# Value products with the values stationary, probabilities divided before they are turned, and a compression in four quadrants

## Chip, core and metric

The kernel runs on one core of a Trainium2 chip. The metric is the device time in microseconds of one launch, the median of three runs; lower is better. The engines are called PE (TensorE), DVE (VectorE), ACT (ScalarE), POOL (GpSimd) and SP (SyncE, which issues the DMAs).

## What is computed

Two transformer blocks on 256 tokens of width 1024, in float32. The change touches the mixer of the first block alone. It projects the tokens, runs three kinds of attention with 4 heads of 64 columns each, and merges them through gates:

```
o_a = stick_breaking(q_a, k_a, v_a)               # w from a suffix sum; o = w @ v, nothing divided
o_b = dsa(q_b, k_b, v_b, index heads)             # o = softmax(scores of chosen keys) @ v_b
kc  = silu(blocks_of_32(k_cmp) @ w1_k) @ w2_k     # 15 blocks of 32 tokens, step 16; vc alike
o_c = g0 * (softmax(q_c kc) @ vc) + g1 * (softmax_sel @ v_sel) + g2 * (softmax_win @ v_win)
merged = sum_j g[j] * (o_j @ w_up[j]);  out = merged @ w_out
```

(silu stands for the gating function of the hidden layer.) The softmax is divided by its sum; whether the division comes before or behind the product with the values is free.

## The kernel before

**Blocks.** The large products run in weight blocks of 256 columns: one DMA of 1 MB into one of four raw buffers, then ACT rounds it to a high part (L1406, "cast", called hi here), DVE subtracts to get the low part (L1742, lo), and PE runs 48 matmuls of 128x128 by 256 (L786 to L788) in two halves of 24. The gate blocks' results are taken from PSUM by DVE (L1753) and then go through a tanh on ACT (L1422), both called the evacuation. The first mixer's blocks are proj 0 to 8, gate 0 to 11, up 0, 2, 1 and out 0 to 3, in that order.

**Order.** Each engine runs a list of steps in one order, written out by hand in `plan()`. A step stands in it once, and each engine that has a part in it does its part at that place of its own row. `between` puts steps between the two halves of a block's matmuls; `evac` comes behind the block and behind the hi and lo of a block that lies two ahead (`ahead`), so DVE evacuates a gate block after it has written another block's lo. Engines meet by semaphores: `fill` tells that a PSUM bank is written, `free` that it is read, and `claim` makes PE wait for a free bank.

**The steps in question.** Units 4 to 11 are the heads of c (query tile t, head h; selected and window keys are two parts of one unit), units 0 to 3 pairs of heads of b. For each, `scores` has PE write logits, DVE mask and take the maximum, and ACT take exponentials and sums (L1593); `turn_p` has PE transpose the probabilities (L1249) and ACT copy them (L1608); `pv` (L1272) multiplies them with the probabilities stationary and 64 value columns moving. `pv_stick` (L1131 to L1133) does so for the stick heads, `cmp_pv` (L1206) for the compressed keys. `o_group` on DVE divides the results and, for c, weighs and adds them (L2134, L2167 to L2195); `turn_o` has PE transpose them (L1286) and ACT and DVE write their high and low parts for the up blocks. `cmp_product` (L1169) is the first layer of the compression: 16 products of a 128-row piece by 16 columns, in two steps of 8 for keys and two for values; `cmp_hidden` on DVE (L2047) and ACT (L1560) is what follows.

**Merging.** After an up block, `merge` on DVE (L2222) weighs its quarter, POOL adds branches (L1691), and `merged_hi`, `merged_lo` (L1631, L2233) split the sum for out 0.

## Time and profile before

| what | us |
|---|---|
| runs | 751.66, 754.02, 752.17 |
| median of the runs | 752.17 |
| span of the profiled execution | 750.7 |

The rows below come from that one profiled execution, whose span is 1.5 us under the median; all times of day in it count from the span's start. The busy time of a group of matmuls ends with the tail of its last one, so the distance between starts is shorter than the busy time divided by the count. A float32 matmul is two instructions.

### The profile page before, as it was taken

The page shows a single profiled execution, that of the slowest core. Times are in us where ns is not written, and L with a number is a line of the kernel's source. Part 1 is how long each engine was busy: PE and PEld are TensorE (multiplying, and loading weights), DVE is VectorE, ACT ScalarE, POOL GpSimd, SP SyncE. Part 2 cuts the span into 40 slices and gives each one's busy share as a digit, 9 for nine tenths or more (in the row PEclk, how much of TensorE's full clock was granted, in tenths as well). Part 3 has the DMA queues.
Part 4 walks back from the last instruction along what each step waited for, and adds up shares of the span by engine and source line. Part 5 has one row for each costly group of instructions (what it writes and reads, how often), then busy time and mean ns, then how long its engine had stood idle before and what let it go on. Part 6 is the DMA issues. An engine that isn't in the chain of part 4 may idle for free.

```text
span 750.7 us, 15016 instructions
## 1 busy us (share of the span) xinstructions
PE 742.7 (99%) x6374; PEld 733.2 (98%) x6374; DVE 601.2 (80%) x897; ACT 376.9 (50%) x506; POOL 30.6 (4%) x22
## 2 busy tenths in 40 slices
PE   8999999999999999999999999999999999999998
PEld 8999999999999999999999999999999999999997
DVE  5756889889897788998998788979787886687554
ACT  6558255745676533443434547356556553434330
POOL 0000000004000000000000000201110000000000
PEclk9999999999999999999999999999999999999999
DMA  9844373342843459999987336655344565678511
GB/s 336 319 153 146 110 275 113 113 139 108 309 174 115 169 173 389 334 349 329 335 306 271 138 127 230 224 174 219 103 173 139 205 224 173 224 281 301 201 58 56
DMA packets 24113, 156.07 MB, mean 208 GB/s; under 512 B 3568, under 2 KB 3696, under 8 KB 6000
## 3 DMA queue, kind: packets, MB, share of 16 engines
q1 hardware_dynamic: 24048, 155.13, 57.6%
q8 instruction: 50, 0.82, 0.4%
q14 instruction: 15, 0.12, 0.0%
HBM read 154.07 MB, written 1.05 MB: 207 GB/s over the span
## 4 chain that ended last, share of the span: by engine, by line
PE 95%; DVE 2%; ACT 1%; DMA 1%; issue 1%; DVEq 0%; SPq 0%
PE bank L786 17%; PE bank L787 16%; PE bank L788 16%; PE bank L867 9%; PE bank L870 9%; PE bank L869 9%; PE bank L794 3%; PE bank L796 3%; PE bank L797 3%; PE bank L1272 2%; PE bank L1239 1%; PE bank L1249 1%; PE bank L1169 1%; DMA sb_raw<-in_stream 1%; PE bank L1322 0%
## 5 line engine op out<-in xcount | busy, mean ns | idle before, releaser
L1742 DVE TENSOR_TENSOR sb_lo<-sb_raw,sb_hi 128x2048 fp32r<-128x2048 f32 (+1 forms) x116 | 261.7, 2259 | 74.5 <-ACT sb_hi L1406 74.1
L1406 ACT CAST sb_hi<-sb_raw 128x2048 fp32r<-128x2048 f32 (+1 forms) x116 | 217.8, 1882 | 100.7 <-PE bank L870 49.3
L786 PE MATMUL bank<-sb_u_hi,sb_hi 128*128 128x256 f32 (+2 forms) x696 | 195.4, 281 | 0.0
L787 PE MATMUL bank<-sb_u_lo,sb_hi 128*128 128x256 f32 (+2 forms) x696 | 192.7, 277 | 0.0
L788 PE MATMUL bank<-sb_u_hi,sb_lo 128*128 128x256 f32 (+2 forms) x696 | 192.6, 277 | 0.0
L786 PEld LDWEIGHTS bank<-sb_u_hi,sb_hi 128*128 128x128 f32 (+2 forms) x696 | 129.6, 186 | 3.0 <-issue 2.2
L787 PEld LDWEIGHTS bank<-sb_u_lo,sb_hi 128*128 128x128 f32 (+2 forms) x696 | 129.8, 186 | 0.3
L788 PEld LDWEIGHTS bank<-sb_u_hi,sb_lo 128*128 128x128 f32 (+2 forms) x696 | 129.7, 186 | 0.2
L867 PE MATMUL bank<-sb_hid_hi,sb_hi 128*128 128x256 f32 x432 | 119.3, 276 | 0.0
L870 PE MATMUL bank<-sb_hid_hi,sb_lo 128*128 128x256 f32 x432 | 119.2, 276 | 0.0
L869 PE MATMUL bank<-sb_hid_lo,sb_hi 128*128 128x256 f32 x432 | 119.2, 276 | 0.0
L786 PE MATMUL bank<-sb_hi,sb_u_hi 128*128 128x256 f32 x320 | 90.9, 284 | 0.0
L787 PE MATMUL bank<-sb_lo,sb_u_hi 128*128 128x256 f32 x320 | 88.8, 277 | 0.0
L788 PE MATMUL bank<-sb_hi,sb_u_lo 128*128 128x256 f32 x320 | 88.8, 277 | 0.0
L869 PEld LDWEIGHTS bank<-sb_hid_lo,sb_hi 128*128 128x128 f32 x432 | 81.1, 188 | 0.0
L867 PEld LDWEIGHTS bank<-sb_hid_hi,sb_hi 128*128 128x128 f32 x432 | 81.1, 188 | 0.0
L870 PEld LDWEIGHTS bank<-sb_hid_hi,sb_lo 128*128 128x128 f32 x432 | 81.1, 188 | 0.0
L786 PEld LDWEIGHTS bank<-sb_hi,sb_u_hi 128*128 128x128 f32 x320 | 60.3, 188 | 0.2
L787 PEld LDWEIGHTS bank<-sb_lo,sb_u_hi 128*128 128x128 f32 x320 | 60.2, 188 | 0.1
L788 PEld LDWEIGHTS bank<-sb_hi,sb_u_lo 128*128 128x128 f32 x320 | 60.1, 188 | 0.0
L2269 DVE SCALAR_TENSOR_TENSOR sb_raw<-sb_raw,sb_c_row 128x1024 f32<-128x1024 f32 x48 | 56.7, 1219 | 0.0
L1444 ACT ACTIVATE sb_act_out<-sb_masked 128x256 f32<-128x256 f32 x22 | 9.1, 418 | 81.8 <-DVE sb_masked L1822 81.8
(368 smaller groups left out, 1330.3 us busy)
## 6 DMA issues: line engine op xcount, KB each, us to landing
sb_raw<-in_stream SPq DMA_DIRECT2D x140, 1024.0 KB, 5.2
sb_raw<-in_stream SPq DMA_DIRECT2D x4, 256.0 KB, 6.6
sb_raw<-in_stream SPq DMA_DIRECT2D x2, 512.0 KB, 8.5
sb_mem_t<-in_mem SPq DMA_DIRECT2D x1, 1024.0 KB, 4.8
out<-sb_h SPq DMA_DIRECT2D x4, 256.0 KB, 2.2
sb_const<-in_constants SPq DMA_DIRECT2D x1, 830.0 KB, 10.8
sb_h<-in_x SPq DMA_DIRECT2D x1, 572.0 KB, 3.6
sb_h<-in_x SPq DMA_DIRECT2D x1, 512.0 KB, 7.0
```

Source lines behind the costliest of these rows:

```text
L786: nc.tensor.matmul(out, a_hi, b_hi, start=(i == 0), stop=False)
L787: nc.tensor.matmul(out, a_hi, b_lo, start=False, stop=False)
L788: last = nc.tensor.matmul(out, a_lo, b_hi, start=False, stop=(i == n - 1))
L794: nc.tensor.matmul(out, a_hi, b_hi, start=(k == 0 and i in opens), stop=False, skip_group_check=True)
L796: nc.tensor.matmul(out, a_hi, b_lo, start=False, stop=False, skip_group_check=True)
L797: last = nc.tensor.matmul(out, a_lo, b_hi, start=False, stop=(k == KD - 1), skip_group_check=True)
L867: nc.tensor.matmul(out, w_hi[:, k, f], x1, start=(first and k == m == 0), stop=False, skip_group_check=True)
L869: nc.tensor.matmul(out, w_hi[:, k, f], x2, start=False, stop=False, skip_group_check=True)
L870: last = nc.tensor.matmul(out, w_lo[:, k, f], x1, start=False, stop=last_one and k == 1, skip_group_check=True)
L1406: nc.scalar.copy(place(hi, s)[:, 0:n], x[:, 0:n]).then_inc(sem("hi_ready"), 1)
L1742: tt(place(lo, s)[:, 0:n], x[:, 0:n], f32(place(hi, s)[:, 0:n]), ALU.subtract) \
L2269: ins = stt(x[:, m, :], x[:, m, :], 1.0, c_row[:, :], ALU.mult, ALU.mult, accum_out=mod[:, 2 * j + m:2 * j + m + 1])
```

## The change

1. Value products (`pv_pair`, `pv_stick`, `cmp_pv`) have 64 value columns stationary and the probabilities moving, two heads in the two column halves of the array. The result is already the transposed output, and `turn_o` on PE goes.
2. Since rows of that result are no longer queries, the division moves ahead: `norm_p` has POOL raise the sums to the power -1 (for c times the gates) and ACT scale each head's probabilities, before `turn_p`. For the compressed keys `turn_cmp_p` on DVE divides. `o_group` for these groups goes.
3. `cmp_product` runs its 16 products in four quadrants of 32 columns with the piece of tokens stationary; ACT copies the result to `cmp_parts`, and `cmp_sum` adds the four with one product by a constant, `pick`, in the middle of the gate block where the second half of the products stood.
4. `turn_o` 0 is taken in gate 2 instead of ahead of gate 6, `turn_o` 2 ahead of up 0, `turn_o` 1 within up 0.

```diff
-    block("gate", 2, between=[("pv_stick", 3), ("o_group", 0), ("turn_cmp", 1), ("index", 0), ("rope1", 3)])
-    steps([("cmp_product", 0, 0)])
-    block("gate", 3, between=[("cmp_product", 0, 1), ("cmp_hidden", 0), ("topk", 0, 0)])
-    steps([("cmp_product", 1, 0), ("topk", 0, 1), ("turn_qk", 2)])
+    block("gate", 2, between=[("pv_stick", 2), ("turn_o", 0), ("turn_cmp", 1), ("index", 0), ("rope1", 3)])
+    steps([("cmp_product", 0)])
+    block("gate", 3, between=[("cmp_sum", 0), ("cmp_hidden", 0), ("topk", 0, 0)])
+    steps([("cmp_product", 1), ("topk", 0, 1), ("turn_qk", 2)])
...
-    steps([("turn_p", 6), ("turn_p", 7), ("scores", 8), ("scores", 9), ("topk", 1, 1), ("split", "gate", 9)])
-    block("gate", 8, ahead=False, evac_now=False, between=[("cmp_pv",), ("o_group", 1)])
+    steps([("turn_p", 6), ("turn_p", 7), ("scores", 8), ("scores", 9), ("norm_p", 8), ("norm_p", 9), ("topk", 1, 1), ("split", "gate", 9)])
+    block("gate", 8, ahead=False, evac_now=False, between=[("cmp_pv",)])
...
     evac(where["gate", 11])
+    add("turn_o", 2)
     split(where["up", 2])
...
+                for k in range(16):
+                    r = slice(32 * (k % 4), 32 * (k % 4) + 32)
+                    pair = 16 * (k - k % 2)
+                    last = nc.tensor.matmul(ps[r, 0:P], cmp_in[:, i, pair:pair + 32], w[:, k, :], start=(k < 4),
+                                            stop=(k >= 12), skip_group_check=True)
+                fill(last, key)
+
+            def cmp_sum(i):
+
+                wait_evacuated(pe, ("cmp_parts", i))
+                ps = claim(("cmp_hidden", i), "turn")
+                fill(nc.tensor.matmul(ps[:, 0:16], cmp_parts[:, i, :], cst("pick"), start=True, stop=True),
+                     ("cmp_hidden", i))
...
+                    for x in (u, u + 1):
+                        i = UNITS[x][2]
+                        r = slice(HD * (i % 2), HD * (i % 2) + HD)
...
+                            out = ps[r, i // 2 * T + t * P:i // 2 * T + t * P + P]
+                            v, p = proj[:, kt, (VSEL, VWIN)[s]:(VSEL, VWIN)[s] + HD], p[:, s, kt, :]
+                        last = nc.tensor.matmul(out, v, p, start=(opens and n == 0), stop=(n == len(parts) - 1),
+                                                skip_group_check=True)
...
+            def cmp_product(i):
+
+                key = ("cmp_parts", i)
+                ps = wait_filled(act, key)
+                free(nc.scalar.copy(cmp_parts[:, i, :], ps[:, 0:P]), key)
...
+            def norm_p(u):
+
+                n = P * (UNITS[u][1] + 1)
+                act.wait_ge(sem("rden_ready"), EXP_ORDER[u] - 3)
+                for m in range(2):
+                    x = prob_of(u)[:, m * n:m * n + n]
+                    last = nc.scalar.activation(x, x, ACT.Copy, scale=rden[:, u, m:m + 1])
+                last.then_inc(sem("p_ready"), 1)
...
+            def norm_p(u):
+
+                pool.wait_ge(sem("exp_done"), EXP_ORDER[u] + 1)
+                kind, t, h = UNITS[u]
+                if kind == "c":
+                    pool.wait_ge(sem("gate_c_halved"), 1)
+                r = rden[:, u, :]
+                ins = nc.gpsimd.tensor_tensor(r, den[:, u, :], minus_one[:, :], ALU.pow)
+                if kind == "c":
+                    link(ins)
+                    ins = nc.gpsimd.tensor_tensor(r, r, gate_c[:, t, h, 1:3], ALU.mult)
+                ins.then_inc(sem("rden_ready"), 1)
...
+                heads = p.rearrange("p (h n) -> p h n", n=32)
+                tt(heads, heads, over(cmp_d[:, :], 32), ALU.mult).then_inc(sem("cmp_p_ready"), 1)
```

The first place is ACT's row around gates 2 to 4, before: the tanh of gate 1 (`sb_gates`), casts, the tanh of gate 2, the hidden unit's tanh (`sb_hid_t`).

```order
L1422 ACTIVATE sb_gates<-sb_gates 128x512
L1406 CAST sb_hi<-sb_raw 128x2048 x2
L1422 ACTIVATE sb_gates<-sb_gates 128x512
L1560 ACTIVATE sb_hid_t<-sb_hid_t 128x15
L1406 CAST sb_hi<-sb_raw 128x2048
L1422 ACTIVATE sb_gates<-sb_gates 128x512
L1529 COPY sb_qk_t<-bank 128x512
L1560 ACTIVATE sb_hid_t<-sb_hid_t 128x15
L1406 CAST sb_hi<-sb_raw 128x2048
```

The same place after:

```order
L1664 ACTIVATE sb_turned_hi<-bank 128x512
L1435 CAST sb_hi<-sb_raw 128x2048
L1451 ACTIVATE sb_gates<-sb_gates 128x512
L1590 COPY sb_prob_t<-bank 128x128
L1595 ACTIVATE sb_hid_t<-sb_hid_t 128x15
L1435 CAST sb_hi<-sb_raw 128x2048
L1451 ACTIVATE sb_gates<-sb_gates 128x512
L1590 COPY sb_prob_t<-bank 128x128
L1558 COPY sb_qk_t<-bank 128x512
L1595 ACTIVATE sb_hid_t<-sb_hid_t 128x15
```

A copy of 128x128 out of PSUM, the partial sums of the compression (`cmp_parts`, kept in `sb_prob_t`), now follows the tanh of gate 2 and another one the tanh of gate 3; the high part of output 0 (`sb_turned_hi`) stands between two casts.

PE waits for that copy. Its row in the middle of gate 3 (the gate's own matmuls are `sb_u_hi`, `sb_u_lo`), before:

```order
L787 MATMUL bank<-sb_u_lo,sb_hi 128x256
L788 MATMUL bank<-sb_u_hi,sb_lo 128x256
L1169 MATMUL bank<-sb_cmp_in,sb_raw 128x16 x8
L786 MATMUL bank<-sb_u_hi,sb_hi 128x256
L787 MATMUL bank<-sb_u_lo,sb_hi 128x256
L788 MATMUL bank<-sb_u_hi,sb_lo 128x256
```

And after:

```order
L790 MATMUL bank<-sb_u_lo,sb_hi 128x256
L791 MATMUL bank<-sb_u_hi,sb_lo 128x256
L1185 MATMUL bank<-sb_const,sb_prob_t 128x16
L789 MATMUL bank<-sb_u_hi,sb_hi 128x256
L790 MATMUL bank<-sb_u_lo,sb_hi 128x256
L791 MATMUL bank<-sb_u_hi,sb_lo 128x256
```

Instead of 8 products of the compression, whose operands are long there, one matmul stands that reads the copy.

The second place is ACT's row around the exponentials of heads 8 and 9 (128x256 x4) and the casts of gates 9 and 10 behind them, before:

```order
L1608 COPY sb_prob_t<-bank 128x256 x2
L1593 ACTIVATE sb_prob,sb_den<-sb_masked,sb_neg_max 128x256 x4
L1406 CAST sb_hi<-sb_raw 128x2048 x2
L1608 COPY sb_prob_t<-bank 128x512 x2
L1593 ACTIVATE sb_prob,sb_den<-sb_masked,sb_neg_max 128x256 x4
L1422 ACTIVATE sb_gates<-sb_gates 128x512
L1406 CAST sb_hi<-sb_raw 128x2048
```

And after:

```order
L1643 COPY sb_prob_t<-bank 128x256 x2
L1628 ACTIVATE sb_prob,sb_den<-sb_masked,sb_neg_max 128x256 x4
L1656 ACTIVATE sb_prob<-sb_prob,sb_rden 128x256 x4
L1435 CAST sb_hi<-sb_raw 128x2048 x2
L1643 COPY sb_prob_t<-bank 128x512 x2
L1628 ACTIVATE sb_prob,sb_den<-sb_masked,sb_neg_max 128x256 x4
L1656 ACTIVATE sb_prob<-sb_prob,sb_rden 128x256 x4
```

Four scalings that need POOL's inverse now stand between the exponentials and the casts, and again ahead of the tanh.

## Rows read from the trace of the kernel before

**Rows 1.** The page's shares of the span: engine, busy us, share, instructions.

```profile
PE 742.7 (99%) x6374; PEld 733.2 (98%) x6374; DVE 601.2 (80%) x897; ACT 376.9 (50%) x506; POOL 30.6 (4%) x22
```

**Rows 2.** Waits of PE (40 to 190 us) and DVE (96 to 190): total, times, longest.

```profile
PE bank L867 <- issue: 0.2, 1, 0.2
...
DVE sb_lo L1742 <- ACT sb_hi L1406: 3.6, 4, 1.2
```

**Rows 3.** PE's list: start us, us (of the group), engine, line, out<-in, count.

```profile
84.56 1.85 PE L1169 MATMUL bank<-sb_cmp_in,sb_raw 128*128 128x16 f32 x16
...
123.05 1.08 PE L1272 MATMUL bank<-sb_proj,sb_prob_t 128*128 128x64 f32 x8
...
131.80 1.03 PE L1206 MATMUL bank<-sb_summed,sb_cmp_in 128*128 128x256 f32 x4
```

**Rows 4.** PE's list, matmuls split by 64 rows.

```profile
127.90 1.13 PE L1227 MATMUL bank<-sb_qk_t 64*128 64x512 f32 x4
...
146.78 0.72 PE L1239 MATMUL bank<-sb_qk_t 64*128 64x128 f32 x8
```

**Rows 5.** ACT's list around gates 2 and 3; brackets: idle before, releaser.

```profile
93.06 0.63 ACT L1422 ACTIVATE sb_gates<-sb_gates 128x512 f32<-128x512 f32 x1 [10.96 <-DVE sb_gates L1753]
...
94.16 1.88 ACT L1406 CAST sb_hi<-sb_raw 128x2048 fp32r<-128x2048 f32 x1
99.07 0.63 ACT L1422 ACTIVATE sb_gates<-sb_gates 128x512 f32<-128x512 f32 x1 [3.03 <-DVE sb_gates L1753]
99.61 0.57 ACT L1529 COPY sb_qk_t<-bank 128x512 f32<-128x512 f32 x1
```

**Rows 6.** DVE's list around gate 2 and the hidden units.

```profile
92.34 0.68 DVE L1753 TENSOR_TENSOR sb_gates<-bank,sb_rstd_bc 128x512 f32<-128x512 f32 x1
92.94 0.16 DVE L2047 COPY sb_hid_x<-bank 128x16 f32<-128x16 f32 x1
...
100.74 0.17 DVE L2047 COPY sb_hid_x<-bank 128x16 f32<-128x16 f32 x1 [0.40 <-PE bank L1169]
```

**Rows 7.** PE by window: us, PE busy (instructions), granted clock, DMA; then one row.

```profile
1.00:4.50 3.50, 3.50 (x16) 1.00 0.75 218
4.50:5.60 1.10, 1.10 (x12) 1.00 0.84 168
8.60:11.60 3.00, 3.00 (x26) 1.00 1.05 427
...
8.50 0.38 PE L794 MATMUL bank<-sb_u_hi,sb_hi 128*128 128x256 f32 x1 [1.98 <-DVE sb_lo L1728]
```

**Rows 8.** ACT's list, exponentials of heads 8 and 9 and the casts behind.

```profile
131.02 0.49 ACT L1593 ACTIVATE sb_prob<-sb_masked,sb_neg_max 128x256 f32<-128x256 f32 x1
131.42 0.19 ACT L1593 ACTIVATION_READ_ACCUMULATOR sb_prob<-sb_masked,sb_neg_max 128x1 f32 x1
...
132.33 0.49 ACT L1593 ACTIVATE sb_prob<-sb_masked,sb_neg_max 128x256 f32<-128x256 f32 x1
...
132.82 3.69 ACT L1406 CAST sb_hi<-sb_raw 128x2048 fp32r<-128x2048 f32 x2
```

**Rows 9.** DVE's list: gate 9's low half.

```profile
134.81 2.29 DVE L1742 TENSOR_TENSOR sb_lo<-sb_raw,sb_hi 128x2048 fp32r<-128x2048 f32 x1 [1.18 <-ACT sb_hi L1406]
```

**Rows 10.** PE's list: first matmuls of gate 9 and of out 0.

```profile
138.37 0.38 PE L786 MATMUL bank<-sb_u_hi,sb_hi 128*128 128x256 f32 x1
...
183.26 0.36 PE L867 MATMUL bank<-sb_merged_hi,sb_hi 128*128 128x256 f32 x1 [0.18 <-issue]
```

**Rows 11.** DVE by window, the work on outputs that goes.

```profile
137.02:139.76 2.74, 2.57 (x8) 1.00 0.59 179
154.70:156.78 2.08, 1.91 (x6) 1.00 0.69 291
168.60:169.72 1.12, 1.05 (x5) 1.00 1.07 453
```

**Rows 12.** POOL's list.

```profile
203.91 0.71 POOL L1683 TENSOR_TENSOR sb_rstd<-sb_mean_square,sb_mhalf 128x2 f32<-128x2 f32 x1 [21.30 <-DVE sb_mean_square L1877]
```

More of the change, by code:

```diff
@@ L98, in constants @@
     put("cmp01", seen)
+    put("pick", (i % 32 - 16 * (i // 32 % 2)) == np.arange(16)[None, :])
     return out
@@ L258, in plan @@
     evac(where["proj", 8])
-    steps([("pv_stick", 1), ("stick", 3), ("split", "gate", 1)])
+    steps([("pv_stick", 0), ("stick", 3), ("split", "gate", 1)])
     block("gate", 0, ahead=False, between=[("turn_qk", 4), ("turn_tail",), ("rounds", "gate", 2)])
@@ L269, in plan @@
+    block("gate", 2, between=[("pv_stick", 2), ("turn_o", 0), ("turn_cmp", 1), ("index", 0), ("rope1", 3)])
+    steps([("cmp_product", 0)])
+    block("gate", 3, between=[("cmp_sum", 0), ("cmp_hidden", 0), ("topk", 0, 0)])
+    steps([("cmp_product", 1), ("topk", 0, 1), ("turn_qk", 2)])
+    block("gate", 4, between=[("cmp_sum", 1), ("cmp_hidden", 1), ("cmp_hid",), ("topk", 0, 2)])
     steps([("index", 1), ("turn_qk", 3)])
     block("gate", 5, between=[("cmp_kv",)])
-    steps([("scores", 4), ("scores", 5), ("topk", 0, 3), ("turn_o", 0)])
+    steps([("scores", 4), ("scores", 5), ("norm_p", 4), ("norm_p", 5), ("topk", 0, 3)])
@@ L272, in plan @@
     block("gate", 6, ahead=False, between=[("cmp_scores",), ("rounds", "gate", 8)])
-    steps([("turn_p", 4), ("turn_p", 5), ("scores", 6), ("scores", 7)])
-    block("gate", 7, ahead=False, between=[("pv", 4), ("pv", 5), ("turn_cmp_p",), ("split", "gate", 8), ("topk", 1, 0), ("turn_qk", 6)])
-    steps([("turn_p", 6), ("turn_p", 7), ("scores", 8), ("scores", 9), ("topk", 1, 1), ("split", "gate", 9)])
-    block("gate", 8, ahead=False, evac_now=False, between=[("cmp_pv",), ("o_group", 1)])
-    steps([("rounds", "gate", 10), ("pv", 6), ("pv", 7), ("turn_p", 8), ("turn_p", 9), ("scores", 10), ("scores", 11)])
+    steps([("turn_p", 4), ("turn_p", 5), ("scores", 6), ("scores", 7), ("norm_p", 6), ("norm_p", 7)])
@@ L278, in plan @@
+    block("gate", 7, ahead=False, between=[("pv_pair", 4), ("turn_cmp_p",), ("split", "gate", 8), ("topk", 1, 0), ("turn_qk", 6)])
+    steps([("turn_p", 6), ("turn_p", 7), ("scores", 8), ("scores", 9), ("norm_p", 8), ("norm_p", 9), ("topk", 1, 1), ("split", "gate", 9)])
+    block("gate", 8, ahead=False, evac_now=False, between=[("cmp_pv",)])
+    steps([("rounds", "gate", 10), ("pv_pair", 6), ("turn_p", 8), ("turn_p", 9), ("scores", 10), ("scores", 11), ("norm_p", 10), ("norm_p", 11)])
     evac(where["gate", 8])
@@ L279, in plan @@
     steps([("split", "gate", 10), ("topk", 1, 2)])
-    block("gate", 9, ahead=False, evac_now=False, between=[("pv", 8), ("pv", 9)])
-    steps([("rounds", "gate", 11), ("turn_p", 10), ("turn_p", 11), ("scores", 0), ("scores", 1)])
+    block("gate", 9, ahead=False, evac_now=False, between=[("pv_pair", 8)])
+    steps([("rounds", "gate", 11), ("turn_p", 10), ("turn_p", 11), ("scores", 0), ("scores", 1), ("norm_p", 0), ("norm_p", 1)])
     evac(where["gate", 9])
     steps([("split", "gate", 11), ("topk", 1, 3)])
-    block("gate", 10, ahead=False, evac_now=False, between=[("pv", 10), ("pv", 11)])
@@ L285, in plan @@
-    steps([("rounds", "up", 0), ("turn_p", 0), ("turn_p", 1), ("scores", 2), ("scores", 3)])
+    block("gate", 10, ahead=False, evac_now=False, between=[("pv_pair", 10)])
+    steps([("rounds", "up", 0), ("turn_p", 0), ("turn_p", 1), ("scores", 2), ("scores", 3), ("norm_p", 2), ("norm_p", 3)])
     evac(where["gate", 10])
     split(where["up", 0])
-    block("gate", 11, ahead=False, evac_now=False, between=[("pv", 0), ("pv", 1)])
+    block("gate", 11, ahead=False, evac_now=False, between=[("pv_pair", 0)])
@@ L2440, in _ @@
                     else:
-                        wait_filled(sp, ("cmp_hidden", before[1]))
+                        wait_filled(sp, ("cmp_parts", before[1]))
                 b = blocks[what[1]] if what[0] == "split" else what
```

175 lines of the change are left out of this document (78 added, 97 removed).

## The prediction

> **What bounds the kernel now.** I read the page's shares first: TensorE (PE) is busy 99% of the span, VectorE (DVE) 80%, ScalarE (ACT) 50% [rows 1]. Then the waits of one engine, in the stretch that the change touches: PE waits 0.2 us in all between 40 and 190 us, DVE some 5 us between 96 and 190 us, most of it for ACT [rows 2]. So both run nearly without a pause, and each step of PE must be asked how long before its use its operand was ready. The lists of single instructions give that. Gate block 0's low half was ready 0.46 us before its use, gate 1's 0.15; gates 2 to 5 have 3.5 to 6.4 us; gate 9 (low half written from 134.81 to 137.10 [rows 9], block begun at 138.37 [rows 10]) 1.3, up 0 1.5; and at out 0 there is none: DVE writes its last piece until 183.16, and PE takes up out 0 at 183.26 after 0.18 us idle [rows 10]. These few narrow places decide. From out 0 on the change touches nothing, so what the kernel gains or loses is the shift of out 0's start, now at 183.26.
>
> **PE's own work.** Removed: value products of 64 columns, where 8 instructions take 1.08 us with the tail of the last, one every 0.115 [rows 3]: 72 for heads b and c, 8.1 us, and 24 for the stick heads, 2.6; twelve transposes of outputs, one every 0.11, 1.3; the compression's four groups of 16 (1.85 with the tail, one every 0.106 [rows 3]), 6.8; its product with the values, 4 instructions of 256 columns at 0.22 (1.03 with the tail [rows 3]), 0.9. Together 19.7. Added: the same sums with 64 value columns stationary and 128 or 256 probabilities moving, two heads in two column halves; compression in 32-column quadrants, four at once; two small sums through `pick`. No product of before is split by columns, so the price has to be bounded. The nearest rows are those split by 64 rows: 4 instructions of 512 take 1.13 us with the tail, and 8 of 128 take 0.72 [rows 4], where the whole array would need 4 times 0.43 for the first by the 0.22 for 256; so their halves run side by side. Each visit to that mode, by the starts before and behind it, costs about 0.42 us more than its work. If column halves overlap alike, the new work is stick 1.3, b 1.3, c 2.6, compression 1.7 and 0.4, the product with the values 0.9, and nine visits 3.7: 12 us, 7.5 us less. If they do not, it is 22 us, 2.3 more. I take the first, since the rows that are nearest overlap. The Trainium skill (TensorEngine Tiling (Array Packing), "Key Properties") says that changing the mode drains the engine; the 0.42 us agrees with that, and its promise of twice and four times the speed by columns would give the 12 us too.
>
> **Where that gain can go.** Not far: up to gate 1 PE may come 0.4 and then 0.1 us earlier before it meets the next low half, which DVE and ACT write no sooner than now. Behind that it meets a new wait.
>
> **The new wait.** The compression's first product is now cut into four partial sums that ACT must copy out of PSUM (`cmp_parts`) before PE adds them up (`cmp_sum`), in the middle of gate 3. PE comes there about 2.82 us (24 matmuls) after gate 3's start: compression begins at 84.5 as now, takes 1.2 instead of 1.7, so it arrives near 88.3. Before, the second half of the products stood there and waited for nothing. But ACT's copy stands behind gate 2's tanh, and that waits for DVE's evacuation of gate 2, which stands behind a 2.29 us low half: DVE evacuates at 92.34, ACT's tanh starts at 93.06 after 10.96 us without work [rows 5, 6]. ACT's next instruction follows 0.54 us after a tanh (99.07 to 99.61 [rows 5]); the copy of 128x128 I take at 0.3 as an exponential of that width. So `cmp_parts` is there at 93.9, and **PE idles from 88.3 to 93.9, 5.6 us**. That alone costs little, as the blocks there have 3.5 us and more in hand and PE saves elsewhere. What costs is who waits behind: DVE's hidden unit, at 92.94 now [rows 6], comes at 94.35, +1.4. ACT's next high half waits for its tanh (94.16 [rows 5]), the low half for that (96.14, after 0.83 idle), and so on to gate 3's evacuation at +1.4. The second compression (arrival 101.5, copy done near 101.3) is even: its hidden unit moves from 100.74 [rows 6] to 101.9, **+1.2**, if PE runs at full speed.
>
> **The clock.** The granted clock reads 1.00 in every stretch, and the pace shows more: at the start, after at least 1 us without work, PE's matmuls go 3.50 us for 16 (0.219), then 1.10 for 12 (0.092) [rows 7], half the pace and then the full one (1.2 and 2.4 GHz); the slow stretch lasts from 0.99 to 4.56 us. The one longer pause inside the kernel, 1.98 us before 8.50, left the pace full (26 in 3.00 us) [rows 7]. A pause of 5.6 us has no row. Bounds: nothing, as after 1.98; or the start's, 3.57 us at half pace, which loses **1.8 us**. I take the second, because the pause is nearly three times the longest that left the clock alone; it is the term I am least sure of. Those 1.8 us fall on gate 3's second half, so PE reaches the second compression sum at 103.3 instead of 101.5, and the second hidden unit comes at 103.5, not 101.9: **+1.6** on DVE, which from there on has hardly a gap to absorb it. The Trainium skill (TensorE: Matmul & The Clock Gate, "The HAM clock gate") warns of exactly such pauses; by it the clock falls to half, by the 1.98 us row alone it would not, and the sum would be 1.6 lower.
>
> **Probabilities divided before they are turned.** For twelve units ACT now multiplies both heads by the inverse (`norm_p`, 24 activations, 0.3 each at 128 wide and 0.4 at 256, the step from 131.02 to 131.42 [rows 8]; some 9 us), and each waits for POOL's power -1. POOL has done little (4%); its 128x2 power takes 0.71 us [rows 12]. For c a multiplication by the gate follows, whose price no row shows: between 0.1 (next to nothing) and 0.7 (as the power); I take 0.4. The wait stands in ACT's row ahead of the next high half, where now the cast follows the exponentials at once (132.33 for 0.49, 132.82 [rows 8]). After the last exponential of a pair: 0.7 + 0.4 + hand-offs 0.2 + two activations, so 1.9 at 128 and 2.1 at 256. For units 4 to 7 ACT has idle time and only the turns of PE wait: +0.5, then +0.3 (shift +1.2, +1.7, +2.0). For units 8, 9 the cast for gate 9 is behind: 132.82 becomes 136.8 (+2.0 and +2.0), its low half ends at 141.1, gate 9 starts at 141.1 and not 138.37, **+2.75**: its 1.3 us are used up.
>
> **What DVE is spared.** The divisions of the outputs go: 2.57 us at 137.02 to 139.76, 1.91 at 154.70, 1.05 at 168.60 [rows 11], and 0.6 before that at 83.59; 0.42 comes back in `turn_cmp_p` (128x256). They lie just behind the delays and pay them back: the shift is +2.1 at scores 0 and 1, +1.45 at gate 11 and up 0. At up 0 the turn of output 2 waits on ACT behind gate 11, and the merges, DVE and POOL (POOL's first addition starts at 175.04), stand in a row to out 0: **+1.4 there**, with the clock held.
>
> **Sum.** +1.4 and +1.6 for the clock: out 0 starts at about 186.3, the span 750.7 becomes 753.7, and on the median of 752.17 (1.5 above the span) **755.2 us**.
>
> **Rivals.** (1) The clock holds: the same idling, no 1.6: 753.6, which is within 0.3% (2.26 us, about what can be told from no change). For it: the 1.98 us row. (2) Column halves run one after the other. Compression products then take 3.5 each, value pairs double; PE has 10 us more than in the forecast and the gates' reserve is gone by gate 9, so about 5 of them show on top: 760. For it: no row has such a split; against: row halves overlap. (3) Faster: ACT's delays are covered and DVE's spared time is what counts. From 112 us on DVE loses 5.5 - 0.4 = 5.1 us of work [rows 11]; against the +1.4 this gives -3.7, 748.5. It decides if gate 9's low half still comes before PE wants it, that is if the round trip through POOL costs under 1.3 us, not 2.0; POOL's 0.71 alone speaks against it. (4) The change doesn't do what it says: the partial copy is ready early because DVE evacuates gate 2 sooner. DVE's row before 92.34 has no gap from 80.33 on, and the change takes one piece of 0.6 us from there and puts one of 0.69 in, so no.
>
> **Chances.** Forecast (idle and slow clock) 0.42, clock holds 0.27, halves in series 0.12, faster 0.12, other 0.07. Each of the first two is uncertain by 1.5 us from POOL's price (three pairs on the path by 0.3) and hand-offs, so the forecast gives some 0.12 of its chance to within 0.3%, the second most. Faster 0.14, the same 0.35, slower 0.51. The range, 749.5 to 759.5, holds the first two with their bounds, half of the faster case and part of the serial one.
>
> **What would show it.** PE idle at the line of `cmp_sum` for about 5.6 us near 88 to 94, released by ACT's copy; its matmuls at 0.21 us behind that for some 3.5 us; `cmp_hidden` at 94.35; ACT waiting for POOL at `norm_p`, and high-half casts right behind; gate 9 near 141 (142.5 with the clock); pairs of value products overlapping (8 instructions of 128 in 0.65 us); from out 0 on the same distances as before. Wrong if PE doesn't stand still at 88, if column halves take 0.11 each in turn, or if DVE is ahead of its old times by 150 us.

## The result, and the profile after

| kernel | median, us | lowest to highest | span of the profiled execution |
|---|---|---|---|
| before | 752.45 (4 runs) | 751.66 to 754.02 | 750.7 |
| changed | 767.43 (4 runs) | 766.27 to 767.87 | 765.8 |

The ratio is 1.0193 [1.0179, 1.0207]: the change makes the kernel 1.9% slower, 15 us. The forecast was 755.2 us with a range up to 759.5. Slower was the likelier side, but the loss is five times the one worked out.

The page of the changed kernel, its first line and the shares, answers to [rows 1]; PE has fewer instructions and is busy 5.6 us longer:

```profile
span 765.8 us, 14997 instructions
...
PE 748.3 (98%) x6346; PEld 732.8 (96%) x6346; DVE 596.5 (78%) x881; ACT 386.2 (50%) x532; POOL 47.6 (6%) x43
```

The waits of PE from 40 to 200 us (engine, line waited for, releaser: total, times, longest), which answer to [rows 2]:

```profile
PE bank L1185 <- ACT sb_prob_t L1590: 5.4, 1, 5.4
...
PE bank L870 <- issue: 1.0, 1, 1.0
PE bank L789 <- DVE sb_lo L1806: 0.9, 1, 0.9
```

The waits of DVE from 96 to 190 us show one that before has not, the 4.2 us for the high part of an output:

```profile
DVE sb_lo L1806 <- ACT sb_hi L1435: 5.2, 3, 3.2
DVE sb_u_lo L1994 <- ACT sb_u_hi L1664: 4.2, 1, 4.2
```

PE's list at the places on which the prediction rested, the compression with its sum, a pair of value products (L1291), gate 9's first matmul and out 0's [rows 3, 10]:

```profile
84.54 1.08 PE L1177 MATMUL bank<-sb_raw,sb_cmp_in 128*32 128x128 f32 x32
...
94.09 0.61 PE L1185 MATMUL bank<-sb_const,sb_prob_t 128*128 128x16 f32 x2 [5.45 <-ACT sb_prob_t L1590]
...
127.29 0.66 PE L1291 MATMUL bank<-sb_prob_t,sb_proj 128*64 128x128 f32 x8
...
144.75 0.36 PE L789 MATMUL bank<-sb_u_hi,sb_hi 128*128 128x256 f32 x1 [0.90 <-DVE sb_lo L1806]
...
190.24 0.36 PE L870 MATMUL bank<-sb_merged_hi,sb_hi 128*128 128x256 f32 x1 [0.99 <-issue]
```

The stall is where it was forecast (5.45 us, released by ACT's copy). All 16 products of one compression (32 instructions) take 1.08 us, where before 8 of them (16 instructions) took 1.85, so quadrants run side by side; the value products' 8 instructions of 128 take 0.66 in two column halves, where 0.65 was forecast. Gate 9 starts at 144.75, not at 142.5, and out 0 at 190.24 instead of 183.26, 6.98 us late and not 3. And then it goes on: the span is 15.1 us longer, so **8.1 us are lost after out 0**, in code that the change does not touch. PE's windows (us, busy and instructions, granted clock, DMA share, GB/s) show both sorts of loss, the slow matmuls behind the stall and a slower pace in the far stretches:

```profile
85.00:88.00 3.00, 3.00 (x44) 1.00 0.69 287
89.00:93.00 4.00, 0.00 (x0) 1.00 0.00 0
...
95.00:99.00 4.00, 4.00 (x21) 0.50 1.00 420
100.00:103.00 3.00, 3.00 (x50) 1.00 0.59 164
...
300.00:400.00 100.00, 100.00 (x870) 1.00 0.91 328
...
747.60:759.60 12.00, 12.00 (x104) 1.00 0.00 1
```

The same two stretches before, the second being the same products of the last layer:

```profile
300.00:400.00 100.00, 100.00 (x885) 1.00 0.91 331
...
733.00:745.00 12.00, 12.00 (x108) 1.00 0.02 6
```

The granted clock is 1.00 in these four rows of the far stretches and PE is never idle in them; each matmul simply takes longer.

### The profile page after: what moved, and what is told of

It reads as the page before. It is cut to its first block, busy times and chain, and to the rows that moved or that the text cites. A ratio compares the mean times of both kernels' runs of the same rounds, so it can differ in the third digit from the quotient of the medians.

```text
span 765.8 us, 14997 instructions
## 1 busy us (share of the span) xinstructions
PE 748.3 (98%) x6346; PEld 732.8 (96%) x6346; DVE 596.5 (78%) x881; ACT 386.2 (50%) x532; POOL 47.6 (6%) x43
## 4 chain that ended last, share of the span: by engine, by line
PE 83%; DVE 8%; ACT 4%; issue 3%; POOL 1%; DMA 1%; DVEq 0%; SPq 0%; ACTq 0%; POOLq 0%
PE bank L789 14%; PE bank L790 13%; PE bank L791 13%; PE bank L870 9%; PE bank L873 9%; PE bank L872 9%; PE bank L797 3%; PE bank L799 3%; PE bank L800 3%; DVE sb_lo L1806 2%; PE bank L1253 1%; PE bank L1314 1%; ACT sb_hi L1435 1%; PE bank L1266 1%; DMA sb_raw<-in_stream 1%
## 5 line engine op out<-in xcount | busy, mean ns | idle before, releaser
L873 PE MATMUL bank<-sb_hid_hi,sb_lo 128*128 128x256 f32 x432 | 121.4, 281 | 0.0
L870 PE MATMUL bank<-sb_hid_hi,sb_hi 128*128 128x256 f32 x432 | 121.3, 281 | 0.0
L872 PE MATMUL bank<-sb_hid_lo,sb_hi 128*128 128x256 f32 x432 | 121.3, 281 | 0.0
```

Source lines behind the costliest of these rows:

```text
L870: nc.tensor.matmul(out, w_hi[:, k, f], x1, start=(first and k == m == 0), stop=False, skip_group_check=True)
L872: nc.tensor.matmul(out, w_hi[:, k, f], x2, start=False, stop=False, skip_group_check=True)
L873: last = nc.tensor.matmul(out, w_lo[:, k, f], x1, start=False, stop=last_one and k == 1, skip_group_check=True)
```

## Experiments: where a tensor lies

The change adds a tensor of 8 bytes (`minus_one`) and 16 constants (64 bytes), and shortens the unused tensor `gap` by 72 bytes of each partition. As written these add up to nothing. The runs fit something else: that all that lies behind `gap` (the projections, merged and mixed tokens, the hidden layers) has moved by 32 bytes, as it would if each tensor's room were rounded up to 32 bytes (64, 32 and 64 less: an estimate, since no address is on record). The weights' high and low parts lie ahead of all three and stay. The few small tensors between the constants and `gap` lie 64 bytes further and were not tried by themselves. The first batch tried the 32 bytes alone, on the kernel before,

```diff
-        sb(ctx, "gap", [P, P // 4])
+        sb(ctx, "gap", [P, P // 4 + 8])
```

> The kernel before, with the tensor gap 8 floats wider, so that every tensor behind it in SBUF (hid_hi, hid_lo, merged_hi, proj, mixed and others) lies 32 bytes further, where the changed kernel has them; nothing else differs, no instruction moves. If the addresses of the operands set the pace of matmuls (0.1133 or 0.118 us from one to the next), this kernel loses what the changed one loses behind out 0: about 7.6 us, 760 us, with the products of sb_hid_hi at 0.118. If the pace hangs on where PE's instructions lie, or on the clock, it stays at 752.2 +- 0.7.

and took it back in the changed kernel:

```diff
-        sb(ctx, "gap", [P, P // 4 - 18])
+        sb(ctx, "gap", [P, P // 4 - 24])
```

> The changed kernel with the tensor gap 6 floats narrower, so that all tensors behind it lie at the addresses that they have in the kernel before. If addresses are the cause of the drift behind out 0, the time falls by about 7.6 us to 759.8, and what is left is the 7 us up to out 0. If they are not, it stays at 767.4.

The kernel before, with nothing but 32 bytes more of unused memory, takes 761.48 us, 1.0112 [1.0097, 1.0127]. The changed kernel with its tensors put back takes 759.89, 1.0089 [1.0073, 1.0106], 7.5 us less than the 767.43 of the changed kernel; its span is 757.7, and beyond out 0 (189.90) it loses 0.4 us instead of 8.1. So half of the loss has nothing to do with the mixer. That the shift was 32 bytes is read from the pace: the products of the hidden layers go one every 0.1182 us in the changed kernel and in this kernel moved by 32 alike, and one every 0.1134 with 6 floats less in `gap`.

A rival was that the pace depends on how the matmuls fall in time and not on addresses; one idle matmul more at the start shifts all that follows:

```diff
-IDLE = {("block", 0): 16, ("mem_o", 0): 3}
+IDLE = {("block", 0): 17, ("mem_o", 0): 3}
```

> The kernel before with one more idle matmul of ones in front (17 instead of 16); all addresses in SBUF as before, all of PE's later instructions one place further in the stream. If the place of PE's instructions decides the pace, whole stretches change between 0.1133 and 0.118 and the time moves by 2 us or more; if addresses decide, it moves by at most 0.3 us: 752.4.

753.09 us against 753.3, ratio 1.0 [0.999, 1.0009]: the time doesn't move.

Which rule of address? Three more distances, all of them the kernel before:

```diff
-        sb(ctx, "gap", [P, P // 4])
+        sb(ctx, "gap", [P, P // 4 + 16])
```

> The kernel before with everything behind gap 64 bytes further (gap 16 floats wider). If what matters is that a moving operand begins at a multiple of 64 bytes, the time stays within 0.5 us of 752.5 and the products of sb_hid_hi keep 0.1133 us. If any other address than the one it was tuned to loses, it costs several us as e1 did (761.5).

```diff
-        sb(ctx, "gap", [P, P // 4])
+        sb(ctx, "gap", [P, P // 4 + 24])
```

> The kernel before with everything behind gap 96 bytes further, again an odd multiple of 32. By the rule of 64 bytes it loses as e1 did, 8 to 9 us: 761, with sb_hid_hi at 0.118. If e1's loss was of that one place, or if the distance to the weights decides, it differs from 761 by 2 us or more.

The theory then was that starts on a multiple of 64 bytes are fast. It fell: a shift by 64 gives 763.67, 1.0151 [1.0135, 1.0166], the slowest of all, and one by 96 gives 758.07, 1.0074 [1.0059, 1.0089]. What was left was the distance between the two operands of a matmul. So in the next kernel everything is moved by 64, the weights' high and low parts too:

```diff
         raw = sb(ctx, "raw", [P, RAW, BLOCK])
+        sb(ctx, "gap_first", [P, 16])
         hi = sb(ctx, "hi", [P, SPLIT * PLACE], F32R)
```

> The kernel before with a gap of 64 bytes ahead of hi, so that the weights (hi, lo) and everything behind them, moving operands too, lie 64 bytes further: their distance from each other is that of before, their start within 128 bytes is not. If the distance between the stationary and the moving operand sets the pace: 752.5 +- 1, sb_hid_hi at 0.1134. If the moving operand's own start does (64 within 128 good, 0 bad, as e13's 0.1198): 763 or more, since sb_u_hi then slows down too.

752.61 against 752.57, 1.0 [0.999, 1.0009]: the same tensors at the same slow address as in the kernel moved by 64, but with the weights moved alike, are fast again. The rows are a stretch of 12 us within the same products, PE alone; moved by 32, by 64, by 96, and all moved by 64:

```profile
742.00:754.00 12.00, 12.00 (x104) 1.00 0.00 0
```

```profile
744.00:756.00 12.00, 12.00 (x102) 1.00 0.00 0
```

```profile
738.20:750.20 12.00, 12.00 (x106) 1.00 0.00 0
```

```profile
733.10:745.10 12.00, 12.00 (x108) 1.00 0.02 6
```

Between starts in PE's list that is, for a product of the hidden layers (`sb_hid_hi`, `sb_hid_lo` moving, the weights stationary), 0.1134 us before, 0.1182 to 0.1184 moved by 32 (the changed kernel too), 0.120 by 64, 0.1167 by 96, and 0.1134 again when both move. So the pace goes with the distance between the moved tensors and those ahead of `gap`, and the stationary operand is the one of these that such a matmul reads; why the distance matters is not shown by any run.

## Experiments: the stall and the clock

Here the changed kernel with its addresses restored is the base. The plan is changed so that ACT copies the partial sums before the tanh of gates 2 and 3, not behind them:

```diff
-    block("gate", 2, between=[("pv_stick", 2), ("turn_o", 0), ...
+    block("gate", 2, evac_now=False, between=[("pv_stick", 2), ("turn_o", 0), ...
     steps([("cmp_product", 0)])
+    evac(where["gate", 2])
-    block("gate", 3, between=[("cmp_sum", 0), ...
-    steps([("cmp_product", 1), ("topk", 0, 1), ("turn_qk", 2)])
+    block("gate", 3, evac_now=False, between=[("cmp_sum", 0), ...
+    steps([("cmp_product", 1)])
+    evac(where["gate", 3])
+    steps([("topk", 0, 1), ("turn_qk", 2)])
```

> As e2 (addresses of before), and in the written order the evacuations of gates 2 and 3 stand behind the compression step, so that ACT copies cmp_parts before it takes the tanh that waits for DVE. PE should then not stand still at cmp_sum (5.4 us in the changed kernel) and keep its full pace. My theory, that this stall puts 3.9 us on the second hidden unit (104.66 against 100.74) and that this is carried to out 0: 3 to 4 us less than e2, 756. Rival, that the delays behind it (POOL, scores) decide: within 1 us of e2.

756.01 us, 1.0039 [1.0024, 1.0054], 3.9 less than its base, though out 0 is only 2.6 earlier in its trace (187.34). The wait at `cmp_sum` is gone and the clock reads 1.00 from 94 to 99. But this need not be the stall's whole price, because the traced execution loses the clock later instead, behind two short waits at the scores of heads 4 and 5:

```profile
112.00:116.00 4.00, 4.00 (x19) 0.50 0.07 10
```

The granted clock averaged over an execution is 0.995 in all four of its base and 0.995, 1.00, 0.998 and 0.995 in the four of the early copy, so in some of them one slow stretch is traded for another. What the second one costs doesn't show in these four: the execution at 1.00 took 756.70 us, the longest. The next kernel leaves the stall and fills it with 26 matmuls on a bank that is free, so that it tells the clock from the lateness:

```diff
             def cmp_sum(i):

-                wait_evacuated(pe, ("cmp_parts", i))
                 ps = claim(("cmp_hidden", i), "turn")
+                stay_warm(ps, 26 if i == 0 else 0)
+                wait_evacuated(pe, ("cmp_parts", i))
```

> As e2 (759.9), with 26 idle matmuls of ones (5.6 us) in PE's pause ahead of the first cmp_sum: the wait stays, only the clock has no reason to fall. In e2 the 24 matmuls behind it run 0.213 us apart instead of 0.115. Theory: 2 to 2.5 us of e2's time is the clock, the rest of the 3.9 us that e3 won is the late hidden unit: 757.6. Rival: the clock costs nothing, since the blocks there have time in hand: 759.5 or more.

757.41 us, 1.0066 [1.0051, 1.0081]. PE's window in the stretch where the changed kernel has 23 instructions at 0.50:

```profile
94.00:99.00 5.00, 5.00 (x67) 1.00 0.93 390
```

The stall is still there (`cmp_sum` runs at 93.76), but the clock isn't lost. Against its base this gives 2.5 us by the medians, 1.7 by the ratios (0.0023, with intervals that overlap) and 2.67 by out 0's start (189.90 to 187.23). The slow stretch itself is measured best in the changed kernel's list: 24 matmuls 0.213 apart, 5.1 us instead of 2.8, so 2.3 lost. Here the clock averages 0.999 or more in all four executions, so this pair of kernels isolates the clock. What remains of the 3.9, about 1.4 us by the medians, is not explained: the two hidden units start at 94.09 and 101.63 with the stall filled and at 93.88 and 101.32 with the early copy, and out 0 comes at the same time in both (187.23 and 187.34). The lateness that ACT's tanh hands on is therefore not measured by itself.

One caution for all comparisons of single traces that follow: the block of 80 columns near 58 us, ahead of everything that these versions differ in, starts anywhere between 57.13 and 58.87 us.

## Experiments: POOL, ACT and DVE behind the pairs

ACT's list around the scaling of heads 8 and 9 in the changed kernel, where [rows 8] had two casts straight behind the exponentials:

```profile
139.51 0.91 ACT L1656 ACTIVATE sb_prob<-sb_prob,sb_rden 128x256 f32<-128x256 f32 x2 [0.28 <-POOL sb_rden L1762]
140.33 3.68 ACT L1435 CAST sb_hi<-sb_raw 128x2048 fp32r<-128x2048 f32 x2
```

The casts start at 140.33; the forecast had 136.8, and some 1.6 more with the slow clock. With the early copy as the base, gate 9's cast is put ahead of the scaling:

```diff
-    steps([..., ("scores", 9), ("norm_p", 8), ("norm_p", 9), ("topk", 1, 1), ("split", "gate", 9)])
+    steps([..., ("scores", 9), ("rounds", "gate", 9), ("norm_p", 8), ("norm_p", 9), ("topk", 1, 1), ("split", "gate", 9)])
```

> As e3, and ACT rounds gate 9's weights (the cast for its high half) before it scales the probabilities of heads 8 and 9, not behind. In e3 that cast starts at 137.4 us against 132.8 before, DVE waits 3.2 us for it, and PE stands 1.6 us at gate 9's start. Theory: the round trip through POOL ahead of this cast is what costs; then gate 9 starts 2 to 3 us earlier and the end comes 1 to 2.5 us earlier than e3 (756.0): 754 to 755. Rival: something behind it (the turn of output 2, the merges) binds anyway: within 0.5 us of e3.

754.94 us, 1.0032 [1.0018, 1.0045]. Out 0 starts at 185.81 instead of 187.34, but the intervals of this kernel and its base overlap: the trace says 1.5 us, of which some 0.8 stand before the second half of gate 8 already (its first matmul at 134.29 against 135.08), ahead of the cast that was moved. The medians can't confirm it.

The other wait is DVE's, at the turn of output 2, which the change puts ahead of the low half of up 2. DVE's list in the changed kernel:

```profile
128.26 2.28 DVE L1806 TENSOR_TENSOR sb_lo<-sb_raw,sb_hi 128x2048 fp32r<-128x2048 f32 x1
...
173.31 0.69 DVE L1994 SCALAR_TENSOR_TENSOR sb_u_lo<-bank,sb_u_hi 128x512 fp32r<-128x512 f32 x1 [4.15 <-ACT sb_u_hi L1664]
173.92 2.28 DVE L1806 TENSOR_TENSOR sb_lo<-sb_raw,sb_hi 128x2048 fp32r<-128x2048 f32 x1
```

DVE stands for 4.15 us with a low half of 2.28 us queued behind it, whose cast on ACT ended at 171.31 (started 169.41, 1.90 long). The order turned round:

```diff
-    add("turn_o", 2)
     split(where["up", 2])
+    add("turn_o", 2)
```

> As e3, and the turn of output 2 stands behind, not ahead of, the high and low half of up 2. In e3 DVE waits 4.2 us for ACT's high part of output 2, with up 2's low half queued behind; out 0 starts 4.1 us late, of which 1.4 arose behind 175 us. Theory: that wait is on the way to out 0; 1 to 2 us less than e3: 754.5. Rival: the wait is only moved, or the merges decide through DVE and POOL: within 0.5 us of e3.

754.29 us, 1.0023 [1.0013, 1.0034]; out 0 at 185.55, 1.8 us earlier than the base. Here too the intervals touch those of the base, and the trace is the clearer witness: the second half of gate 8 starts at 134.98 against 135.08, so nearly all of the 1.8 us arises behind it.

What does the inverse cost? Without it (POOL computes nothing; ACT still makes every scaling, by ones; the division and the gates of selection and window are left out, so the output is another one):

```diff
-                act.wait_ge(sem("rden_ready"), EXP_ORDER[u] - 3)
+                act.wait_ge(sem("exp_done"), EXP_ORDER[u] + 1)
...
-                    last = nc.scalar.activation(x, x, ACT.Copy, scale=rden[:, u, m:m + 1])
+                    last = nc.scalar.activation(x, x, ACT.Copy, scale=ones[:, 0:1])
```

> As e3, but POOL takes no inverse at all and ACT multiplies the probabilities by one without a wait for POOL: the division of the softmax and the gates of the selected and window parts are left out, so the output differs. It shows what the wait for POOL costs, with ACT's 24 scalings kept. Theory: most of e3's 3.8 us over the kernel before: 753. Rival: ACT's own scalings (9 us) and DVE's waits cost it: 755.5 or more.

752.76 us, 1.0005 [0.9994, 1.0016], out 0 at 182.61: without the round trip the changed mixer is level with the old one. So ACT's scalings cost nothing that shows, and the wait for POOL does: 3.2 us by the medians, 2.6 by the ratios. The 4.7 us at out 0 say too much, since the traced execution is the quickest of ten (751.25) and keeps its clock where that of the base loses it:

```profile
112.00:116.00 4.00, 4.00 (x38) 1.00 0.19 31
```

Over all executions the clock differs less: two of the ten average 0.995 (754.95 and 754.27 us), the other eight 0.997 to 1.00 (751.25 to 752.94). POOL's list in the changed kernel says where the wait is long. The rows are the power and the multiplication by the gate; DVE's row above at 128.26 is a low half:

```profile
127.49 0.70 POOL L1759 TENSOR_TENSOR sb_rden<-sb_den,sb_minus_one 128x2 f32<-128x2 f32 x1 [4.98 <-ACT sb_prob L1628]
128.27 2.33 POOL L1762 TENSOR_TENSOR sb_rden<-sb_rden,sb_gate_c 128x2 f32<-128x2 f32 x1
...
131.33 0.20 POOL L1762 TENSOR_TENSOR sb_rden<-sb_rden,sb_gate_c 128x2 f32<-128x2 f32 x1
...
147.91 2.19 POOL L1762 TENSOR_TENSOR sb_rden<-sb_rden,sb_gate_c 128x2 f32<-128x2 f32 x1
```

The same operation on 128x2 takes 0.20 us alone and 2.33 when it starts 0.01 us after a low half on DVE; it ends when that ends (130.54 for DVE, 130.60 for POOL). At 147.91 DVE's low half has run since 147.76, and it is so again. ACT's row shows what each pair waits, from the end of the last exponential to the end of the last scaling: 2.0 us for heads 4 and 5, 4.2 for heads 6 and 7, behind the stretched one at 128.27, and 2.1 for heads 8 and 9. The row of heads 6 and 7 begins

```profile
130.63 0.70 ACT L1656 ACTIVATE sb_prob<-sb_prob,sb_rden 128x128 f32<-128x128 f32 x2 [2.45 <-POOL sb_rden L1762]
```

The Trainium skill (SBUF — State Buffer, "Who interferes with whom") says that a DVE instruction with two inputs in SBUF and a GpSimd instruction that reads SBUF exclude each other, and that the second one is blocked until the first ends; the trace agrees with 2.33 us against 0.20. That rule was there to be read and was not weighed.

Whether DVE should then do it, reciprocal and multiplication, was tried on the version of the next section that has all three repairs:

```diff
+            def norm_p(u):
+
+                dve.wait_ge(sem("exp_done"), EXP_ORDER[u] + 1)
...
+                ins = nc.vector.reciprocal(r, den[:, u, :])
+                if kind == "c":
+                    link(ins)
+                    ins = tt(r, r, gate_c[:, t, h, 1:3], ALU.mult)
+                ins.then_inc(sem("rden_ready"), 1)
```

> As e10, with the inverse (and the gates' product) of norm_p taken by DVE, a reciprocal and a multiplication of 128x2 at 0.17 to 0.2 us, in place of POOL's power at 0.70 and its multiplication, which takes 0.2 or, beside a low half on DVE, up to 2.3 us. Theory: the round trip is shorter by 0.5 us for each pair and by 2 where POOL is held up: 1 to 2 us less than e10. Rival: DVE now stands in its row until ACT's exponentials are done, and its low halves come later: 1 us or more above e10.

756.06 us, 1.0049 [1.0034, 1.0063], against 1.0015 for its base. DVE's waits from 100 to 190 us:

```profile
DVE sb_rden L2214 <- ACT sb_prob L1631: 6.6, 9, 2.0
```

DVE is fuller than POOL, and in its row the small step stands still for ACT's exponentials, 6.6 us in nine waits. One of DVE's late steps also reaches PE, and behind it 9 matmuls of the gate block go some 0.21 us apart, at the lower clock:

```profile
127.44 0.69 PE L1217 MATMUL bank<-sb_const,sb_cmp_in 128*128 128x128 f32 x2 [3.40 <-DVE sb_cmp_in L2170]
```

All four executions average 0.995 to 0.998, against 0.999 or more for the base, so the 2.3 us between them are waits and clock together. POOL's interference is the smaller evil.

## Experiments: each half alone, and all together

Only the compression in quadrants, in the kernel before, with the early copy and the addresses of before (the rest as in the change's third item):

```diff
-                x = cmp_in[:, i, :].rearrange("p (k n) -> p k n", k=16)
-                for k in half(16, part):
-                    last = nc.tensor.matmul(ps[:, 0:16], w[:, k, :], x[:, k, :], start=(k == 0), stop=(k == 15))
...
+                for k in range(16):
+                    r = slice(32 * (k % 4), 32 * (k % 4) + 32)
+                    pair = 16 * (k - k % 2)
+                    last = nc.tensor.matmul(ps[r, 0:P], cmp_in[:, i, pair:pair + 32], w[:, k, :], start=(k < 4),
+                                            stop=(k >= 12), skip_group_check=True)
```

> The kernel before with only the compression in four quadrants (cmp_parts, cmp_sum), the copies ahead of the tanh as in e3, and all tensors of the large products at the addresses of before; values and probabilities as before. PE saves 4.3 us there, but it is DVE that binds behind it. Theory: no gain beyond 0.5 us, 752 to 752.7, as the low halves come no earlier. Rival: the saving shows at the end, 749 to 751.

754.38 us, 1.0025 [1.0012, 1.0038], above what either theory had. It is not faster, although PE does less. PE's list, at the scores of heads 4 and 5:

```profile
109.12 0.70 PE L1240 MATMUL bank<-sb_qk_t 64*128 64x256 f32 x2 [1.09 <-ACT sb_qk_t L1538]
...
110.73 1.22 PE L1240 MATMUL bank<-sb_qk_t 64*128 64x256 f32 x2 [0.92 <-DVE sb_work L2028]
```

PE comes there early and stands twice, and behind that its window reads

```profile
112.00:116.00 4.00, 4.00 (x20) 0.50 0.17 27
```

where the kernel before has 38 instructions at 1.00. Out 0 comes at 186.60, 3.3 late. So 12 idle matmuls were put ahead of gate 5, the block before it:

```diff
-IDLE = {("block", 0): 16, ("mem_o", 0): 3}
+IDLE = {("block", 0): 16, ("block", 14): 12, ("mem_o", 0): 3}
```

> As e8 (quadrants alone, 754.4), plus 12 idle matmuls of ones (2.6 us) ahead of gate 5, which give PE back the time that the quadrants save. In e8 PE comes early to the scores of heads 4 and 5, stands there for about 2.7 us in two pieces, and the granted clock falls to 0.50 for some 5 us behind it. Theory: it is that clock that makes the faster compression lose; with PE kept busy it stays full and the time is 751.5 to 752.7 although PE does more. Rival: the loss of e8 is elsewhere (order of the evacuations on ACT and DVE): 754 or more.

```profile
112.00:116.00 4.00, 4.00 (x38) 1.00 0.38 104
```

The trace is as expected, full pace and out 0 at 183.44. The median is not: 753.72, 1.0022 [1.0013, 1.0031]. The 3.2 us of the one trace are 0.7 in the medians, with intervals that overlap. The clock of whole executions says why: of the six of the quadrants alone, the two at 0.994 took 755.86 (the traced one) and 755.41 us, the other four, at 0.998 to 1.00, 752.79 to 754.60. With the idle matmuls all ten read 0.999 or more and took 752.91 to 754.90. So the clock falls that far in some executions only. That the kernel with its clock kept, idle matmuls included, is still 1.3 us above the kernel before by the medians stays without a cause.

The value products alone, with the cast and the turn of output 2 in the repaired order, and the compression as before:

```diff
-    steps([("cmp_product", 0)])
-    block("gate", 3, evac_now=False, between=[("cmp_sum", 0), ("cmp_hidden", 0), ("topk", 0, 0)])
+    steps([("cmp_product", 0, 0)])
+    block("gate", 3, between=[("cmp_product", 0, 1), ("cmp_hidden", 0), ("topk", 0, 0)])
```

> As e10, but with the compression of before (no quadrants, no cmp_parts) and without the idle matmuls of e9: the value products with the values stationary and the scaling ahead of the turn alone, with the cast ahead of the scaling and the turn of output 2 behind the low half. PE is 4.3 us less relieved, so it should not idle at the scores of heads 4 and 5. Theory: what is left of e10's 1.3 us over the kernel before is the path through POOL and ACT: 753 to 754. Rival: the value part is neutral and the rest is the quadrants': 752 to 752.6.

753.64 us, 1.0014 [1.0004, 1.0023]; out 0 at 183.91. All three repairs of the changed kernel together, with the 12 idle matmuls:

```diff
+    evac(where["gate", 2])
...
-    steps([..., ("scores", 9), ("norm_p", 8), ...
+    steps([..., ("scores", 9), ("rounds", "gate", 9), ("norm_p", 8), ...
...
-    add("turn_o", 2)
     split(where["up", 2])
+    add("turn_o", 2)
...
+IDLE = {("block", 0): 16, ("block", 14): 12, ("mem_o", 0): 3}
```

> The changed kernel with addresses of before, the copy ahead of the tanh (e3), the cast ahead of the scaling (e5), the turn of output 2 behind the low half (e6), and the 12 idle matmuls of e9. Sum of the parts: 756.0 less 1.1, 1.7 and 2.5 for the clock: 750.7. Rival: the parts share one path, and POOL's delays (up to 2.4 us for an operation) keep it at 752 to 753.

753.8 us, 1.0015 [1.0006, 1.0025], out 0 at 183.34. Both branches of the expectation are missed, the sum of the parts (750.7) by 3.1 us. And the same without the idle matmuls:

```diff
-IDLE = {("block", 0): 16, ("block", 14): 12, ("mem_o", 0): 3}
+IDLE = {("block", 0): 16, ("mem_o", 0): 3}
```

> As e10 (753.8) without the 12 idle matmuls: quadrants, value products, the copy, the cast and the turn moved. If the fall of the clock behind the scores of heads 4 and 5 matters here, this is 1 us or more slower than e10 and its runs spread over 2 us or more; if the path through POOL and ACT decides, it is within 0.5 us of e10.

754.08 us, 1.0018 [1.0009, 1.0028], out 0 at 184.17. This is within 0.5 us of the version with them, the second branch of the expectation. The same two waits stand in its list,

```profile
109.06 0.70 PE L1244 MATMUL bank<-sb_qk_t 64*128 64x256 f32 x2 [1.10 <-ACT sb_qk_t L1557]
...
110.67 0.70 PE L1244 MATMUL bank<-sb_qk_t 64*128 64x256 f32 x2 [0.91 <-DVE sb_work L2079]
```

and the clock stays at 1.00 from 106 to 118 us. Yet over its ten executions it averages from 0.995 to 1.00, so the same kernel with the same waits keeps its clock in one execution and not in another. Two short waits are not enough to predict a fall. No version is faster than the kernel before: with all repairs in, out 0 starts where it did (183.34 and 184.17 against 183.26), and what is taken from PE buys nothing.

## Why the prediction was right and where it was wrong

**Right.** The stall: place, releaser and size (5.6 forecast, 5.45 measured), from ACT's row of the kernel before; the early copy removes it. The clock does fall after it, which no row of before showed. Quadrants and column halves overlap: the 32 instructions of one compression take 1.08 us where in turn they were put at 3.5, and 8 instructions of a pair 0.66 where in turn they would take some 1.0. So the rival "halves in series" is out. "Faster" is too: its own condition, a round trip through POOL under 1.3 us and not 2.0, is missed (2.0 to 4.2). ACT's scalings, as such, cost nothing that shows.

**"From out 0 on the change touches nothing."** This step failed, and it carries half of the loss: 7.5 us by the medians, 8.1 in the traces. It was drawn from the list of instructions, which is indeed unchanged there. The addresses are not. The diff showed `minus_one`, `pick` and the new length of `gap`, so the question could have been asked; but their sizes as written cancel, and neither the shift nor its price could be read from any row of before.

**The clock's price.** Taken from the start of the kernel as 1.8 us, with some 3.5 us of slow matmuls; 24 matmuls 0.213 apart are 5.1 us and lose 2.3. The two hidden units came at 94.73 and 104.66, where 94.35 and 103.5 were forecast. Filling the stall gives back 2.5 us by the medians, where the forecast had 1.6 for this at out 0. The early copy gives back 3.9, although some of its executions lose the clock later on; the forecast had 3.0 for the whole change.

**POOL's round trip.** The multiplication was bounded by 0.1 and 0.7 and taken as 0.4. Alone it takes 0.20, inside; beside a low half 2.19 and 2.33, far outside: the lower bound had no row, and the upper one came from a power with DVE idle beside it [rows 12]. The forecast had 1.9 us from the last exponential to the last scaling for heads 6 and 7, and it was 4.2. For heads 8 and 9, just ahead of gate 9's cast, it had 2.1, and that is what it was; but their exponentials end at 138.34, 1.9 us later than the forecast's sum gives (132.82 + 2.0 + 1.6). That this is the 2.2 us lost one pair earlier, and so most of the 2.25 us by which gate 9 missed the forecast, is likely and not isolated by a run. What is shown is that the kernel without the inverse is faster than its base.

**The turn of output 2.** Its new place was named in the change and was priced at nothing. DVE waits there 4.15 us with a low half queued behind, and undoing it moves out 0 by 1.8 us. The rule to "name what is queued behind the waiting instruction" was applied to `norm_p` and `cmp_sum`, and not to this one.

By size, in ratios: 0.0104 of the 0.0193 are addresses (7.8 us; 7.5 by the medians), 0.0050 is what the early copy gives back (3.8), net of the clock lost later in some executions, and the remaining 0.0039 (2.9 us) the wait for POOL, the turn of output 2 and, in some executions, the clock at 112 us. The last three overlap on the path, so that their single effects (about 3, 1.8, up to 3) don't add up, and no run separates them fully.

## What to carry to other kernels

A change that adds or resizes a tensor also moves every tensor behind it, here although the sizes as written cancelled: work out the new addresses and hold them fixed while you judge the rest, since here 32 bytes cost 1.1% by themselves. Before a small step goes to GpSimd or behind a wait, look at what runs at that moment on DVE and what is queued behind the waiting instruction; the lone duration of the step is no bound. And where another engine sets the pace, work taken from PE comes back as idle time, which can cost more than the work did once the clock falls.

## What the runs showed of the hardware

- The pace of matmuls of 128x128 by 256 on the high and low parts changes with where the moving operand lies while the stationary one stays: for the hidden layers 0.1134 us as before, 0.1182, 0.120 and 0.1167 with the moving one 32, 64 and 96 bytes further, and 0.1134 when both are moved by 64. The mechanism is open. Also open is a second effect of like size on one matmul: with addresses unchanged, the products of the output blocks (from 183.26 us on) go one every 0.1178 us in the kernel before and mostly one every 0.1133 in the early-copy kernel (from 187.34 on).
- A 128x2 multiplication on POOL goes from 0.20 to 2.33 us when it starts beside a 2.28 us subtraction of two SBUF operands on DVE; a 128x2 power that starts at 165.90, with such a subtraction under way since 165.21, takes 2.14 instead of 0.70.
- After 5.45 us without work PE ran 24 matmuls at 0.213 us (granted 0.50, the 1.2 GHz level), and was at full pace again from 99.93 us on. Two waits of 1.09 and 0.92 us, 1.6 apart, were followed by 0.50 or 0.57 in four traces (the quadrants alone, the early copy, and the two kernels with one repair more) and by 1.00 in two (no inverse; all three repairs). It isn't the kernel alone that decides: executions of either of these two average from 0.995 to 1.00. What else does is open.
- Products on 32 columns in four quadrants overlap in float32: 16 products, 32 instructions of 128 columns moving, in 1.08 us with the tail.
